# Rows of 520 columns for the second stage's input blocks, and the shift columns of the opening computed by matmuls

## The reference

```python
def rms_norm(x, g):
    xf = x.astype(jnp.float32)
    y = xf * lax.rsqrt(jnp.mean(xf * xf, axis=-1, keepdims=True) + EPS)
    return (y * g.astype(jnp.float32)).astype(x.dtype)

# first block
mod = jax.nn.silu(c) @ w_ada[layer] + b_ada[layer]          # 1024 -> 3 * 1024
shift, scale, gate = jnp.split(mod[:, None, :], 3, axis=-1)
h = rms_norm(x, norm_g[layer]) * (1.0 + scale) + shift
proj = h @ w_in[layer]
(hq, hf, hi, hz, rq, rk, rv, rz, ga, gb) = jnp.split(proj, offsets, axis=-1)
# HGRN2 heads from hq, hf, hi, hz; retention heads from rq, rk, rv, rz; gated by ga, gb -> m
x = x + gate * (m @ w_out[layer])                            # then an RMS norm

# second block, 2 layers: conformer convolution | banded attention, each with a SwiGLU FFN
h = h + conformer_conv(rmsnorm(h, norm_mix[l]), ...)
h = h + attn @ w_o[j]
h = h + swiglu_ffn(rmsnorm(h, norm_ffn[l]), ffn_w_up[l], ffn_w_down[l])
```

## Time and profile before

| | us |
|---|---|
| median of 3 runs | 1711.39 (1709.36 to 1718.76) |
| the profiled execution | 1709.66 |
| its span, first to last instruction | 1707.9 |
| PE busy | 1640.8 (96%) |
| DVE busy | 821.4 (48%) |
| ACT busy | 773.1 (45%) |
| POOL busy | 734.0 (43%) |
| mean granted TensorE clock | 0.989 |

### The profile page before, as it was taken

How to read it: one execution, slowest core, us unless ns; L and a number is a source line. 1 busy time by engine, 2 the same in 40 slices (tenths; PEclk the granted TensorE clock), 3 DMA queues, 4 the chain that set the end, 5 groups by cost and what they waited for, 6 DMA issues and landing times.

```text
span 1707.9 us, 21958 instructions
## 1 busy us (share of the span) xinstructions
PE 1640.8 (96%) x7922; PEld 1339.2 (78%) x7922; DVE 821.4 (48%) x1380; ACT 773.1 (45%) x1157; POOL 734.0 (43%) x316
## 2 busy tenths in 40 slices
PE   4899999999999999989999999999999999999997
PEld 2787887887887778848888888888787888888885
DVE  6875575575575549986321221226465221121123
ACT  4554554554554665765442222236575542222232
POOL 3343353343343426863444444445223444444442
PEclk7999999999999999999999999999999999999999
DMA  9232332332332346302233222233112223223221
GB/s 381 89 103 68 101 105 67 99 100 71 99 101 70 125 75 172 99 25 74 87 98 99 98 98 98 93 97 118 63 50 65 96 92 105 90 95 107 90 98 62
DMA packets 49875, 167.58 MB, mean 98 GB/s; under 512 B 4987, under 2 KB 9500, under 8 KB 49308
## 3 DMA queue, kind: packets, MB, share of 16 engines
q1 hardware_dynamic: 43696, 154.50, 27.1%
q10 hardware_dynamic: 6124, 12.33, 3.0%
HBM read 161.56 MB, written 5.24 MB: 98 GB/s over the span
## 4 chain that ended last, share of the span: by engine, by line
PE 79%; DVE 11%; ACT 3%; issue 3%; POOL 2%; DMA 1%; ACTq 0%; DVEq 0%; POOLq 0%; SPq 0%
PE gps L1458 22%; PE gps L1460 22%; PE gps L1459 22%; DVE aps L1309 4%; POOL w_lo L471 2%; DVE ada_w L993 1%; PE gps L1504 1%; PE gps L1506 1%; PE gps L1505 1%; DMA w_raw<-weights_dram 1%; PE aps L1644 1%; PE aps L1792 1%; PE aps L1572 1%; PE aps L1650 1%; PE aps L1802 1%
## 5 line engine op out<-in xcount | busy, mean ns | idle before, releaser
L471 POOL TENSOR_TENSOR w_lo<-w_raw,w_hi 128x1024 fp32r<-128x1024 f32 x260 | 662.4, 2551 | 923.8 <-ACT w_hi L548 923.7
L1458 PE MATMUL gps<-xa_hi,w_hi 128*128 128x512 f32 x1128 | 452.2, 401 | 21.0 <-POOL xa_lo L478 13.0
L1460 PE MATMUL gps<-xa_hi,w_lo 128*128 128x512 f32 x1128 | 441.5, 391 | 0.0
L1459 PE MATMUL gps<-xa_lo,w_hi 128*128 128x512 f32 x1128 | 441.5, 391 | 0.0
L548 ACT CAST w_hi<-w_raw 128x1024 fp32r<-128x1024 f32 x260 | 270.6, 1043 | 152.0 <-PE gps L1460 133.9
L1458 PE MATMUL gps<-xb_hi,w_hi 128*128 128x512 f32 x736 | 288.3, 392 | 2.5 <-POOL w_lo L471 1.3
L1460 PE MATMUL gps<-xb_hi,w_lo 128*128 128x512 f32 x736 | 286.5, 389 | 0.0
L1459 PE MATMUL gps<-xb_lo,w_hi 128*128 128x512 f32 x736 | 286.4, 389 | 0.0
L1458 PEld LDWEIGHTS gps<-xa_hi,w_hi 128*128 128x128 f32 x1128 | 213.2, 189 | 74.3 <-issue 18.8
L1459 PEld LDWEIGHTS gps<-xa_lo,w_hi 128*128 128x128 f32 x1128 | 213.5, 189 | 45.0 <-issue 3.1
L1460 PEld LDWEIGHTS gps<-xa_hi,w_lo 128*128 128x128 f32 x1128 | 213.1, 189 | 45.4
(11 more groups left out here) (263 smaller groups left out, 1994.1 us busy)
## 6 DMA issues: line engine op xcount, KB each, us to landing
w_raw<-weights_dram SPq DMA_DIRECT2D x268, 512.0 KB, 3.2
ada_w<-ada_in_dram SPq DMA_DIRECT2D x8, 1024.0 KB, 15.7
gates<-ret_tab_dram ACTq DMA_DIRECT2D x4, 1024.0 KB, 5.6
rel_scratch_dram<-rel_rows ACTq DMA_DIRECT2D x1, 3072.0 KB, 33.8
x<-x_turned_dram SPq DMA_DIRECT2D x2, 1024.0 KB, 9.7
res<-xT_dram ACTq DMA_DIRECT2D x1, 2048.0 KB, 8.4
bias<-rel_scratch_dram ACTq DMA_DIRECT2D x1, 2048.0 KB, 8.4
outT_dram<-y SPq DMA_DIRECT2D x8, 256.0 KB, 2.1
```

The costliest lines, as they stand in the source:

```text
L471: TT(w_lo[:, j, :], w_raw[:, j, :], w_hi[:, j, :].bitcast(F32), ALU.subtract).then_inc(lo_ready[j], 1)
L1458: mm(gps[:, j, :], w_hi[:, j, w], x[0][:, k, :], start=k == 0, stop=False)
L1459: mm(gps[:, j, :], w_hi[:, j, w], x[1][:, k, :], start=False, stop=False)
L1460: last = mm(gps[:, j, :], w_lo[:, j, w], x[0][:, k, :], start=False, stop=k == blocks - 1)
```

## The change

There are two edits, in one program.

The first: `xb_hi` and `xb_lo` are allocated with rows of 520 columns, of which 512 are used. Block `k` then starts at 128 + 32 k modulo 256. Both still start at 128 modulo 256, and what lies behind them moves by 256 or 512 bytes.

The second is in the opening. The shift half of `ada_w` comes from the host in the layout of a weight chunk, and TensorE multiplies it by silu(c) as a column (`c_col`), read 128 times over by a step of zero: eight float32 matmuls of 128 columns for one block's shift column, into one of four places in PSUM. ScalarE adds `b_ada` to one column of it. The shift is no longer added in place: ScalarE rounds `hbuf` + shift straight to `xa_hi`, and VectorE computes `xa_lo` = (`hbuf` + shift) - `xa_hi` for all eight blocks, in one instruction each. VectorE's reductions are halved in number, and GpSimd has only weights. `x0` is loaded whole ahead of `ada_w`, and TensorE's order is written out anew. The new tile `c_col` moves the tiles of the first stage behind it by 64 bytes.

```diff
-        xb_hi = sb("xb_hi", [P, KC, T], F32R, where=second)
-        xb_lo = sb("xb_lo", [P, KC, T], F32R, where=second)
+        xb_hi = sb("xb_hi", [P, KC, T + BLOCK_PAD], F32R, where=second)[:, :, 0:T]
+        xb_lo = sb("xb_lo", [P, KC, T + BLOCK_PAD], F32R, where=second)[:, :, 0:T]
...
+        shift_at = [aps[:, 1, 0:P], aps[:, 2, 0:P], aps[:, 3, 0:P], gps[:, 3, 0:P]]
...
+            for c in range(2):
+                k = slice(c * KC // 2, (c + 1) * KC // 2)
+                sp.dma_start(x0[:, k, :], x_turned.rearrange("(k p) t -> p k t", p=P)[:, k, :]).then_inc(x_in[c], 16)
             for c in range(KC):
-                if c < 2:
-                    k = slice(c * KC // 2, (c + 1) * KC // 2)
-                    sp.dma_start(x0[:, k, :], x_turned.rearrange("(k p) t -> p k t", p=P)[:, k, :]).then_inc(x_in[c], 16)
                 sp.dma_start(ada_w[:, 2 * c:2 * c + 2, :], ada_in[2 * c:2 * c + 2].rearrange("c p k -> p c k"))\
                   .then_inc(ada_loaded[c], 16)
-                if 2 <= c < 5:
-                    load(0, c - 2)
+                if c in (2, 4, 6):
+                    load(0, c // 2 - 1)
...
-            for c in range(KC - LAST_LOW):
-                if c < 3:
-                    w_low(0, c)
-                pool.wait_ge(xh_ready, c + 1)
-                TT(xa_lo[:, c, :], hbuf[:, c % 4, :], xa_hi[:, c, :].bitcast(F32), ALU.subtract).then_inc(x_ready, 1)
+            for c in range(3):
+                w_low(0, c)
...
             for c in range(KC):
-                if c < 3:
-                    w_high(0, c)
+                if c in (0, 3, 6):
+                    w_high(0, c // 3)
+                act.wait_ge(shift_full, c + 1)
+                own.mark(nc.scalar.activation(mod[:, c:c + 1], shift_at[c % len(shift_at)][:, 0:1], ACT.Identity, bias=vcol("b_ada", c)))
                 act.wait_ge(h_ready, c + 1)
-                own.done(nc.scalar.activation(hbuf[:, c % 4, :], hbuf[:, c % 4, :], ACT.Identity, bias=mod[:, c:c + 1]))
-                nc.scalar.copy(xa_hi[:, c, :], hbuf[:, c % 4, :]).then_inc(xh_ready, 1)
+                own.wait()
+                nc.scalar.activation(xa_hi[:, c, :], hbuf[:, c % 4, :], ACT.Identity, bias=mod[:, c:c + 1]).then_inc(xh_ready, 1)
...
+            gain_at = {c: modulation(c) for c in range(3)}
+            for c in range(3):
+                scaled_input(c)
             for c in range(KC):
-                modulation(c)
-
-                if c >= 2:
-                    for n in range(0, 3) if c == 2 else (c,):
-                        scaled_input(n)
-            for c in range(KC - LAST_LOW, KC):
+                if c + 3 < KC:
+                    gain_at[c + 3] = modulation(c + 3)
                 input_low(c)
+                if c + 3 < KC:
+                    scaled_input(c + 3)
...
+            def shift(c):
+
+                pe.wait_ge(ada_loaded[c], 16)
+                if c >= len(shift_at):
+                    pe.wait_ge(xh_ready, c - len(shift_at) + 1)
+                for k in range(KC):
+                    last = mm(shift_at[c % len(shift_at)], ada_w[:, 2 * c + 1, k * P:(k + 1) * P], c_col[:, 0, k:k + 1].to_broadcast([P, P]),
+                              start=k == 0, stop=k == KC - 1)
+                last.then_inc(shift_full, 1)
...
+            for c in range(5):
+                shift(c)
+            opening(0, 0, 3)
+            shift(5)
+            opening(0, 3, 4)
+            shift(6)
+            opening(1, 0, 4)
+            shift(7)
+            for c in range(2):
+                opening(c, 4, 6)
+            opening(2, 0, 6)
+            for k in range(6, KC):
                 for c in range(3):
-                    dense(START["pairs"], c, xa, operand=x_wait(X_MIX) if c == 0 else None, part=(k, k + 1))
-            for c in range(3):
-                dense(START["pairs"], c, xa, operand=x_wait(X_MIX) if c == 0 else None, part=(KC - 3, KC))
+                    opening(c, k, k + 1)
```

More of the change, by code:

```diff
@@ L218, in program @@
         lbt = sb("lbt", [P, 4, KC], where=first)
+        c_col = sb("c_col", [P, 2, KC], where=first)
         gate_sum = sb("gate_sum", [P, 2], where=first)
@@ L306, in program @@
         lb_exp = sem("lb_exp")
[L307 removed]
+        c_sig = sem("c_sig")
+        c_col_ready = sem("c_col_ready")
+        shift_full = sem("shift_full")
         sq_ready = sem("sq_ready")
@@ L991, in modulation @@
                 dve.wait_ge(ada_loaded[c], 16)
-                for n, col in ((2 * c, KC + c), (2 * c + 1, c)):
-                    own.mark(nc.vector.tensor_tensor_reduce(
-                        ada_w[:, n, :], ada_w[:, n, :], c_wide[:, 0, :], op0=ALU.mult, op1=ALU.add, scale=1.0,
-                        scalar=vcol("b_ada", col), accum_out=mod[:, col:col + 1]))
-                own.wait()
-                own.mark(STT(mix_gain[:, c:c + 1], mod[:, KC + c:KC + c + 1], 1.0, vcol("norm_g", c), ALU.add, ALU.mult))
+                col = KC + c
+                own.done(nc.vector.tensor_tensor_reduce(
+                    ada_w[:, 2 * c, :], ada_w[:, 2 * c, :], c_wide[:, 0, :], op0=ALU.mult, op1=ALU.add, scale=1.0,
+                    scalar=vcol("b_ada", col), accum_out=mod[:, col:col + 1]))
+                own.mark(STT(mix_gain[:, c:c + 1], mod[:, col:col + 1], 1.0, vcol("norm_g", c), ALU.add, ALU.mult))
+                return own.local
             def scaled_input(c):
@@ L1004, in scaled_input @@
                     dve.wait_ge(x_ready, c - 3)
-                own.wait()
+                own.wait(gain_at[c])
                 STT(hbuf[:, c % 4, :], x0[:, c, :], mix_gain[:, c:c + 1], rstd[:], ALU.mult, ALU.mult).then_inc(h_ready, 1)
@@ L1010, in input_low @@
                 dve.wait_ge(xh_ready, c + 1)
-                dve.wait_ge(x_ready, c)
-                TT(xa_lo[:, c, :], hbuf[:, c % 4, :], xa_hi[:, c, :].bitcast(F32), ALU.subtract).then_inc(x_ready, 1)
-            for c in range(KC):
-                modulation(c)
-                if c >= 2:
-                    for n in range(0, 3) if c == 2 else (c,):
-                        scaled_input(n)
-            for c in range(KC - LAST_LOW, KC):
+                STT(xa_lo[:, c, :], hbuf[:, c % 4, :], mod[:, c:c + 1], xa_hi[:, c, :].bitcast(F32), ALU.add, ALU.subtract)\
+                    .then_inc(x_ready, 1)
+            gain_at = {c: modulation(c) for c in range(3)}
+            for c in range(3):
+                scaled_input(c)
+            for c in range(KC):
+                if c + 3 < KC:
+                    gain_at[c + 3] = modulation(c + 3)
                 input_low(c)
+                if c + 3 < KC:
+                    scaled_input(c + 3)
             own.done(nc.vector.tensor_copy(silu_c, c_wide[:, 0, :]))
@@ L1538, in _, with opening @@
                 sum_squares(RMS_MIX, c)
-            for k in range(KC - 3):
+            def shift(c):
[6 more added lines that the diff above has]
+                last.then_inc(shift_full, 1)
+            def opening(c, k0, k1):
+                dense(START["pairs"], c, xa, operand=x_wait(X_MIX) if c == 0 else None, part=(k0, k1))
+            pe.wait_ge(c_col_ready, 1)
+            for c in range(5):
[10 more added lines that the diff above has]
+            for k in range(6, KC):
                 for c in range(3):
-                    dense(START["pairs"], c, xa, operand=x_wait(X_MIX) if c == 0 else None, part=(k, k + 1))
-            for c in range(3):
-                dense(START["pairs"], c, xa, operand=x_wait(X_MIX) if c == 0 else None, part=(KC - 3, KC))
+                    opening(c, k, k + 1)
             def pair(p):
@@ L1927, in ada_chunks @@
 def ada_chunks(w_ada):
-    order = [n for c in range(KC) for n in (KC + c, c)]
-    return np.stack([np.ascontiguousarray(w_ada[:, c * P:(c + 1) * P].T) for c in order])
+    return np.stack([m for c in range(KC) for m in (np.ascontiguousarray(w_ada[:, (KC + c) * P:(KC + c + 1) * P].T),
+                                                    chunk(w_ada[:, c * P:(c + 1) * P]))])
 def token_order():
```

9 lines of the change are left out of this document (7 added, 2 removed).

## The result

The changed kernel takes 1719.98 us (median of six runs, 1716.6 to 1721.24), the kernel before 1711.41 (1709.36 to 1718.76, six runs): the ratio is 1.0041, 95% interval 1.0024 to 1.0057. It is slower, where 1707.6 us was forecast, and above the range of 1700 to 1719. By the medians the difference is 8.6 us. The ratio, over all executions, says less, 7.0 us (4.1 to 9.8); one of the six of before took 1718.76. The profiled execution took 1721.24 us against 1709.66, 11.6 more; its span is 1719.4 us.

What follows compares the result with a forecast made beforehand. TensorE, busy 96% of the span, was taken to bound the kernel through matmul pace and waits. 1709.66 - 3.8 (opening) + 0 (padded rows) = 1705.9, plus 1.73 to the median: 1707.6 us; range 1700 to 1719.

Steps and rivals of the forecast that it cites:

- I take 0: Cost of padded xb rows in 1932 matmuls: put at 0, between bounds of -25.7 and +13.7 us.
- The rows of 520: Prediction's section on xb products reading padded rows: 2208 matmuls, 1932 starting elsewhere modulo 256, net effect 0.
- rival A: xb products: moving operands starting unlike the stationary ones modulo 256 cost up to 7.1 ns, 1721.3 us; chance 0.19.
- Its mean is above 226.7, so distance alone hardly frees the 13.3: Convolution's wandering operand, 233.8 ns a matmul: argument against unlike starts removing the 13.3 ns over 213.3 ns array time.
- The opening, up to the logarithm: Program start to ScalarE's forget-gate logarithm: chunk 3 ends at 63.6 us, logarithm starts at 67.5 instead of 71.27, 3.8 earlier.
- Later: After the logarithm: chain 3.8 us early, TensorE waits 2.3 us instead of 0.65 before first heads; three pairs repeat as before.
- B: xb products: padding gains, the 13.3 ns being colliding operand reads, gone in 7 of 8: 1681.9 us; chance 0.09.
- C: Opening: shifts 0 to 4 keep the clock up, so 2.0 us are not lost: 1705.6 us; chance 0.12.
- D: Opening: shifts take 3.5 us each throughout, the three on the path cost 5.1 more: 1712.7 us; chance 0.10.

Runs made afterwards that it cites:

- experiment 2: Rows of 520 columns for xb_hi and xb_lo alone, in the kernel before: 1723.65 us beside 1712.1, ratio 1.0067.
- experiments 3 and 4: Kernel before, rows of 512, all xb blocks moved alike, to 160 and to 0 modulo 256: 1727.64 and 1723.9 us, one execution each.
- experiment 1: The changed kernel's opening alone, xb rows of 512 columns again: 1708.98 us beside 1712.1 for the kernel before, ratio 0.9981.
- experiment 5: Kernel before with xb_hi rows of 576 columns and a shorter filler, all blocks still at 128 modulo 256: 1710.7 us beside 1712.7, one execution.
- experiment 9: Kernel of experiment 8 with TensorE's opening reordered: shifts 5 to 7 earlier, chunks 0 and 1 together before chunk 2: 1701.42 us beside 1712.72, ratio 0.9934.
- experiments 9 and 10: Experiment 9, and its kernel without holding back GpSimd's w_lo of chunk 11: the latter 1700.44 us beside 1712.39 for the kernel before, ratio 0.9929.
- experiment 8: Kernel of experiment 1 with GpSimd's w_lo of chunk 11 held back in the first pair until VectorE's products are done: 1707.28 us beside 1712.72, ratio 0.9964.

## Why the prediction was wrong

**The step that failed** is "I take 0" under "The rows of 520". The term was put at 0 between bounds of -25.7 and +13.7 us; measured were 2208 x (232.72 - 227.19) = 12.2 us in the trace, and 11.6 in the medians of experiment 2. The one row with unlike starts was the right one to go by: the convolution's pace of 233.8 ns is close to that of all `xb` products once their starts are unlike (232.2 to 233.6 in five kernels). That the convolution's own pace comes from its starts is not shown; no run moved its operands. The mechanism was in the list as rival A, with "7.1 ns" as its price and 1721.3 us as its time, against 1719.98 measured; what was wrong was its chance of 0.19. Of the two reasons held against it, one (the convolution's starts move by 4 bytes, within a line) is answered by experiments 3 and 4, where distances of 32 and 128 bytes cost about the same 6 ns; the other (VectorE works on PSUM all the while) by the `xb` products, where VectorE is busy for 29% of the time (860 to 1240 us). "Its mean is above 226.7, so distance alone hardly frees the 13.3" was sound, and should have been followed to its end: a row in which all distances occur and none is cheap is evidence for a cost. And A itself was a little off: not 7 blocks in 8 pay, but all (block 0 too, at 231.1 ns), and 5.5 ns in the mean instead of 7.1.

The prediction took from the Trainium skill's SBUF — State Buffer, SBUF: two separate sides, and Advanced Engine Details and Errata, SBUF Cachelines, that steps of 32 bytes would do nothing. This is not borne out: the runs show 5.5 ns a matmul. What the pages state, that TensorE's ports wait for no other engine and that SBUF has lines of 16 bytes, no run here contradicts; neither names a cost of how TensorE's own two operands lie to each other, and the measurement decides.

**The opening, up to the logarithm, went as written.** Shift columns of 1.8 us as 16 records (5.52 for 48); the sums over at 18.5 (18.3); block 0's `xa_lo` at 27.8 (27.7), block 1's at 32.5 (33.0), block 2's at 35.2 (35.8); two short visits of TensorE between 28 and 36; clock at 0.56 there; none waited for after 36; the logarithm at 67.46 (67.5); the heads' first wait 1.58 us (2.3). Two small things were off. ScalarE read chunk 3's result at 64.30 us instead of 63.6, since the clock came back at 41.5 and not at 40. And the last load of `ada_w` landed at 36.6, not at 34.6, which held nothing up: its reduction began at 38.52. The 64 bytes by which the first stage's tiles moved show as less than 0.2 us in experiment 1's trace, from 100 to 550 us.

**What the step "Later" missed.** It lets the chain pass the first heads as early as it comes to them, and this does not hold behind a shared turn. The chain came 3.8 us earlier to the first heads and left them 1.3 us earlier: TensorE waited 2.14 us longer in front of their second part (2.72 against 0.58), since GpSimd's `w_lo` had the turn in between; the second part then took 4.13 us instead of 2.50, most of it at 1.2 GHz; and 1.25 us less lie between its end and chunk 10, 1.00 us of which is the wait for `w_lo` that stood there, the rest an overlap of the modelled end: -3.83 + 2.14 + 1.63 - 1.25 = -1.3. The granted clock of that stretch and of the one in which the rest went:

```profile
80.00:100.00 20.00, 15.69 (x90) 13.98 (x89) 17.39 (x31) 12.89 (x18) 7.49 (x3) 0.91 0.41 131
220.00:230.00 10.00, 7.13 (x48) 6.97 (x48) 9.10 (x9) 3.80 (x6) 6.72 (x3) 0.83 0.51 159
```

Both stretches are at 1.00 in the kernel before. A clock of 0.83 over 10 us leaves out 1.7 us of work, which is the step from -1.3 to +0.3 in the table: TensorE's 256-column matmuls stand 0.21 us apart there instead of 0.12. Ahead of it is a wait of 2.87 us for `w_lo`; the kernel before has the same wait in the same place (2.85 us) and no fall behind it, so what decides is not this wait alone, and stays open.

This wait is the turn again, and the program doesn't fix it. In the seven traces with the opening of before, four pairs each, TensorE waits in front of chunk 10 either 1.00 us (15 times, with waits of 0.5 to 0.8 us in front of both parts of the heads in addition) or 2.85 us (13 times), from none of the four pairs in experiment 5 to all four in experiment 2, though the first stage is the same program. Over all twelve traces, 16 of the 20 waits of 2.84 to 2.87 us have a fall of the clock at them, and none of the 25 waits of 1.00 us has. But for one such fall the pairs of the changed kernel's trace do repeat as before. By the medians the opening keeps 3.1 us (experiment 1), so not every execution loses them; how often the clock takes its part can't be told from one profile of each.

**Rivals B, C and D.** B: no gain anywhere, in no run are unlike starts faster at 512 columns. C: the clock was up from 20 to 30 us (1.00), but not from 30 to 40; experiment 9 shows what it would have taken, work for TensorE between the blocks. D: a shift takes 1.8 us at 2.4 GHz; shift 5 takes 3.6 us in a stretch with a granted clock of 0.56.

## What to carry to other kernels

A buffer that a tuned matmul reads has a place: in a stream of float32r matmuls of 512 columns like this one, keep the moving and the stationary operand at the same address modulo 256, all of them, and look at where every later tile ends up before a pad is put in. Price an unknown by the row in the trace that has the suspected property, not by a value between the bounds that no row has. And where two engines take turns, an instruction that comes earlier can come into the other's turn: what a faster opening is worth is read at the far end of that queue.

## What the runs showed of the hardware that I had not expected

- A stream of float32r matmuls of 512 columns went at 226.7 ns where all have their two operands at the same place modulo 256, and slower at every other distance tried: 32 and 128 bytes cost 6.4 and 6.0 ns each, one product of three at another place makes all three slower (231.7, 233.7 and 230.2), and a joint move costs nothing (227.19).
- In the products of 256 columns it is the other way round: the 96 with `xb` stand 119.9 ns apart at like starts, and 118.3 to 118.7 at unlike ones, in five kernels. It is worth 0.1 us here and was tried with no others.
- With short pieces of work between the waits the clock stayed up: in experiments 9 and 10 the granted clock is 1.00 from 20 to 50 us with TensorE busy for 8.1 to 9.0 us of each ten up to 40, where it is 0.56 from 30 to 40 us in the changed kernel, with waits of 3.79 and 1.07 us. Behind the first heads a wait of 1.61 us was followed by a fall (experiment 8), and one of 0.66 was not (experiment 9). The length of one wait doesn't decide: 2.85 us were followed by a fall in most places and not in others.
- VectorE and GpSimd take turns here, and which of them goes first at the same place in the program differs from pair to pair and from kernel to kernel, with first stages that are the same (13 of 28 pairs one way).
